# Inner channels of an expert in one block of 512 and three of 1024, on bias rows and a ring of six pieces

## The reference

```python
h = rms_norm(x, g_mix[l])
u = jnp.einsum('bsd,dc->bsc', h, w_in[l])
# three token mixers: pooling, convolution of 31 taps, forgetting attention of 8 heads
logf = jax.nn.log_sigmoid(f_logit)
c = cumsum(logf, axis=1)
s = einsum(q_i, k) * scale + (c_q - c_k)          # bias from the forget gates
s = where(kpos <= qpos, s, -inf); o = softmax(s) @ v
x = x + einsum(merged, w_out[l])
# channel mixer: layer 0 dense SwiGLU (2816 inner channels),
# layer 1 the two best of eight experts (3584 inner channels each)
out = out + gates[..., e:e + 1] * (silu(h @ w1[e]) * (h @ w3[e])) @ w2[e]
```

## Time and profile before

| | us |
|---|---|
| time, median of 3 runs | 1668.14 (1666.18 to 1669.09) |
| the profiled execution, its own time | 1673.39 |
| its span, first to last instruction | 1671.5 |
| TensorE busy in the span | 1634.1 (98%) |
| VectorE busy | 1290.0 (77%) |
| ScalarE busy | 1056.3 (63%) |
| mixer of layer 0, dense layer | about 0 to 230, 230 to 430 |
| mixer of layer 1, experts | about 430 to 645, 645 to 1671 |

### The profile page before, as it was taken

One profiled execution on the slowest core, in us unless ns is written; L12 is line 12 of the kernel. 1 busy time (PEld: TensorE's weight loads), 2 busy tenths in 40 slices (PEclk: granted clock), 3 DMA queues, 4 the chain that ended last, 5 costly groups with the idle time before them and its releaser, 6 DMA issues.

```text
span 1671.5 us, 25101 instructions
## 1 busy us (share of the span) xinstructions
PE 1634.1 (98%) x9644; PEld 1433.8 (86%) x9644; DVE 1290.0 (77%) x1097; ACT 1056.3 (63%) x908; POOL 61.9 (4%) x60
## 2 busy tenths in 40 slices
PE   7999989999899998999999999999999999999998
PEld 7998989999898897888888888888888888888887
DVE  5973764444697476897997998997988987987986
ACT  5444444454554454677777777777777777777775
POOL 0121100000012110000000000000000000000000
PEclk9999999999999998999999999999999999999999
DMA  9543455556454343799999999999999999999993
GB/s 335 167 146 106 127 167 171 191 175 200 126 170 133 103 133 120 258 377 369 327 374 354 344 371 340 358 372 334 365 371 333 363 375 334 359 377 334 359 377 132
DMA packets 231294, 452.48 MB, mean 271 GB/s; under 512 B 6992, under 2 KB 80720, under 8 KB 231120
## 3 DMA queue, kind: packets, MB, share of 16 engines
q1 hardware_dynamic: 231248, 451.82, 76.7%
HBM read 450.74 MB, written 1.05 MB: 270 GB/s over the span
## 4 chain that ended last, share of the span: by engine, by line
PE 93%; DVE 4%; ACT 2%; issue 1%; DMA 0%; ACTq 0%; DVEq 0%
PE bank L278 28%; PE bank L280 27%; PE bank L279 27%; PE bank L1292 2%; PE bank L1308 1%; DVE w_low L268 1%; PE bank L1326 1%; ACT w_high L264 1%; PE bank L1041 1%; PE bank L1129 1%; DVE h_full L628 1%; DVE rinv L618 0%; PE bank L1131 0%; PE bank L1148 0%; PE bank L1092 0%
## 5 line engine op out<-in xcount | busy, mean ns | idle before, releaser
L268 DVE TENSOR_TENSOR w_low<-raw,w_high 128x2048 fp32r<-128x2048 f32 x427 | 977.8, 2291 | 284.4 <-ACT w_high L264 283.2
L264 ACT ACTIVATE w_high<-raw 128x2048 fp32r<-128x2048 f32 x427 | 818.9, 1919 | 378.1 <-PE bank L280 376.7
L278 PE MATMUL bank<-w_high,hg_high 128*128 128x512 f32 x896 | 354.5, 396 | 0.7 <-issue 0.7
L280 PE MATMUL bank<-w_high,hg_low 128*128 128x512 f32 x896 | 350.1, 391 | 0.0
L279 PE MATMUL bank<-w_low,hg_high 128*128 128x512 f32 x896 | 349.3, 390 | 0.0
L278 PE MATMUL bank<-h_high,w_high 128*128 128x256 f32 x1056 | 301.8, 286 | 6.4 <-DVE h_low L623 4.8
L280 PE MATMUL bank<-h_high,w_low 128*128 128x256 f32 x1056 | 295.3, 280 | 0.0
L279 PE MATMUL bank<-h_low,w_high 128*128 128x256 f32 x1056 | 295.3, 280 | 0.0
L278 PEld LDWEIGHTS bank<-h_high,w_high 128*128 128x128 f32 x1056 | 200.8, 190 | 11.8 <-issue 9.4
L279 PEld LDWEIGHTS bank<-h_low,w_high 128*128 128x128 f32 x1056 | 199.1, 189 | 1.6 <-issue 1.4
L280 PEld LDWEIGHTS bank<-w_high,hg_low 128*128 128x128 f32 x896 | 168.6, 188 | 36.0
(11 more groups left out here) (242 smaller groups left out, 1586.6 us busy)
## 6 DMA issues: line engine op xcount, KB each, us to landing
raw<-exp_w SPq DMA_DIRECT2D x336, 1024.0 KB, 5.3
raw<-w_in SPq DMA_DIRECT2D x42, 1024.0 KB, 5.1
raw<-ffn_w SPq DMA_DIRECT2D x33, 1024.0 KB, 5.3
raw<-w_out SPq DMA_DIRECT2D x8, 1024.0 KB, 4.9
raw<-w_br_attn SPq DMA_DIRECT2D x4, 1024.0 KB, 5.0
raw<-w_br_pool SPq DMA_DIRECT2D x2, 1024.0 KB, 5.2
raw<-w_br_conv SPq DMA_DIRECT2D x2, 1024.0 KB, 4.9
cst<-consts SPq DMA_DIRECT2D x1, 1280.0 KB, 13.4
```

What stands on the lines that cost most here:

```text
L264: nc.scalar.activation(wh[c % SPLIT][:], raw[c % RAW][:], ACT.Copy).then_inc(s["high_done"], 1)
L268: nc.vector.tensor_tensor(wl[c % SPLIT][:], raw[c % RAW][:], wh[c % SPLIT][:].bitcast(F32), ALU.subtract).then_inc(s["split_done"], 1)
L278: pe.matmul(dst, lh, rh, start=start and i == 0, stop=False)
L280: last = pe.matmul(dst, ll, rh, start=False, stop=stop and i == len(terms) - 1)
```

## The change

It has three parts.

Bias rows: DVE writes the negated log forget gates of both token tiles into a zeroed tile nlf, twice (for high and low rows). PE sums them over the tokens with three fp32 matmuls, bias_sums, after piece 8. ACT and DVE make high and low rows of it in the tile crow. For each head one fp32r matmul with a broadcast column of sel8 adds the row to all queries; the term of the query falls out of the softmax. The mask is added in fp32r. POOL only zeroes tiles. The head's division moves up by one piece, and ten of the convolution's operations move ahead of other work.

Ring of six: w_low takes the memory of raw, so that DVE subtracts in place, and w_high has six tiles too. The load of piece c waits for used of piece c - 6; the high part waits for the load alone.

Wide expert blocks: block 0 of a job has 512 inner channels, and three more have 1024. Up pieces of a wide block have two row chunks by 1024 columns. A wide block takes two banks for w1 (0 and 5), two for w3 (1 and 6), two for the turns (4 and 7), and four down pieces. The work tiles of the experts lie over the tile h_full. The transposes of the permutation move to the start of the last block, and all of a job is written out on PE, ACT, DVE and SP, without an inner loop.

```diff
-RAW = 6
-SPLIT = 3
+RING = 6
...
+WIDE = 3
...
-GATHER_BANKS = (5, 6, 7, 0)
-TAPS_AT = {4: 6, 5: 6, 6: 1, 7: 1, 8: 1, 9: 1, 10: 8, 11: 8, 12: 8, 13: 8, 14: 7, 15: 7}
+GATHER_BANKS = (0, 5, 1, 6)
+COMBINE_BANKS = (5, 4, 6, 7)
+TURN_BANKS = (4, 7)
+TAPS_AT = {4: 6, 5: 6, 6: 1, 7: 1, 8: 1, 9: 1, 10: 8, 11: 8, 12: 6, 13: 5, 14: 5, 15: 4}
+TAPS_AHEAD = {12: 2, 13: 3, 14: 2, 15: 3}
...
-        raw = [sb(f"raw{i}", [P, PIECE]) for i in range(RAW)]
-        wh = [sb(f"w_high{i}", [P, PIECE], F32R) for i in range(SPLIT)]
-        wl = [sb(f"w_low{i}", [P, PIECE], F32R) for i in range(SPLIT)]
+        with ExitStack() as loaded:
+            raw = [loaded.enter_context(nc.sbuf_tensor(f"raw{i}", [P, PIECE], F32)) for i in range(RING)]
+        wl = [sb(f"w_low{i}", [P, PIECE], F32R) for i in range(RING)]
+        wh = [sb(f"w_high{i}", [P, PIECE], F32R) for i in range(RING)]
...
         def load_piece(sp, c, r, src, k):
-            if not (isinstance(r, int) and c < RAW):
-                sp.wait_ge(s["split_done"], num(c - RAW + 1, r))
-            sp.dma_start(fold(raw[c % RAW][:], k), src).then_inc(raw_in[c % RAW], 16)
+            if not (isinstance(r, int) and c < RING):
+                sp.wait_ge(s["used"], num(c - RING + 1, r))
+            sp.dma_start(fold(raw[c % RING][:], k), src).then_inc(raw_in[c % RING], 16)
 
         def split_high(act, c, r=0):
...
-            if not (isinstance(r, int) and c < SPLIT):
-                act.wait_ge(s["used"], num(c - SPLIT + 1, r))
...
+                def bias_sums():
+                    pe.wait_ge(s["nlf_in"], 2 * l + 2)
+                    pe.wait_ge(s["qk_root"], 4 * l + 3)
+                    pe.matmul(bank[6][0:64, 0:128], nlf[:, 0, :], C(C_UPTO), start=True, stop=True)
+                    pe.matmul(bank[6][0:64, 128:384], nlf[:, 0, :], C(C_UPTO, 2), start=True, stop=False)
+                    pe.matmul(bank[6][0:64, 256:384], nlf[:, 1, :], C(C_UPTO), start=False,
+                              stop=True).then_inc(s["bias_sum"], 1)
...
-                    pe.matmul(B[:, 0:128], q[:, 0:P], k[:, 0:P], start=True, stop=False)
-                    pe.matmul(B[:, 0:128], decay[:, h % 2, 0, :], C(C_AFTER), start=False, stop=False)
-                    pe.matmul(B[:, 0:128], ident, C(C_MASK), start=False, stop=True)
-                    pe.matmul(B[:, 128:384], q[:, P:S], k, start=True, stop=False)
-                    pe.matmul(B[:, 128:256], decay[:, h % 2, 2, :], C(C_AFTER), start=False, stop=False)
-                    pe.matmul(B[:, 128:384], decay[:, h % 2, 1, :], C(C_ONES, 2), start=False, stop=False)
-                    pe.matmul(B[:, 256:384], ident, C(C_MASK), start=False, stop=True).then_inc(s["scores"], 1)
+                    pe.matmul(B[:, 0:384], sel8[:, h:h + 1].to_broadcast([P, P]), crow[:], start=True, stop=False)
+                    pe.matmul(B[:, 0:128], identr[:], maskr[:], start=False, stop=False)
+                    pe.matmul(B[:, 256:384], identr[:], maskr[:], start=False, stop=False)
+                    pe.matmul(B[:, 0:128], q[:, 0:P], k[:, 0:P], start=False, stop=False)
+                    pe.matmul(B[:, 128:384], q[:, P:S], k, start=False, stop=True).then_inc(s["scores"], 1)
...
+                def up(c, r, banks, kn):
+
+                    for k0 in range(0, KC, kn):
+                        H, L = take_piece(pe, c, r, kn)
+                        for a, b in enumerate(banks):
+                            f = slice(512 * a, 512 * a + 512)
+                            ins = products(pe, bank[b][:], [
+                                (hgH[:, k0 + k, :], hgL[:, k0 + k, :], H[:, k, f], L[:, k, f]) for k in range(kn)],
+                                start=k0 == 0, stop=k0 + kn == KC)
                         ins.then_inc(s["used"], 1)
...
+                    for i in range(WIDE):
+                        if i == WIDE - 1:
...
+                        pe.wait_ge(s["m_silu"], r0 + (2 * i + 1))
+                        if i == 0:
                             pe.wait_ge(s["m_add"], j * 4 + 1)
...
+                        c = up(c, r0, (0, 5), 2)
...
+                        turn(r0 + (2 * i if i else 1), 2 if i else 1)
...
+                        c = up(c, r0, (1, 6), 2)
+                        c = down(c, r0, r0 + (2 * i if i else 1), 2 if i else 1, start=i == 0)
+                    turn(r0 + 2 * WIDE, 2)
                     pe.wait_ge(s["m_silu"], r0 + EXP_BLOCKS)
...
                     for g in range(4):
                         gather(g)
...
+                    down(c, r0, r0 + 2 * WIDE, 2, stop=True)
```

More of the change, by code:

```diff
@@ L220, in trunk @@
         x_in = [sem(f"x_in{m}") for m in range(4)]
-        raw_in = [sem(f"raw_in{i}") for i in range(RAW)]
+        raw_in = [sem(f"raw_in{i}") for i in range(RING)]
         def C(i, n=1):
@@ L560, in job @@
                     if not isinstance(j, int):
-                        for k in range(SPLIT):
+                        for k in range(3):
                             split_high(act, c + k, r0)
@@ L585, in experts @@
+                    split_high(act, c + 3, r0)
                 job(0)
@@ L976, in job @@
                     r0, c = j * EXP_BLOCKS, MOE0
-                    for k in range(SPLIT if isinstance(j, int) else 0, 4):
+                    for k in range(3 if isinstance(j, int) else 0, 4):
                         split_low(dve, c + k, r0)
@@ new lines, in job @@
+                    for i in range(WIDE):
+                        for k in range(0 if i else 2, 6):
+                            split_low(dve, c + k, r0)
+                            if i == 0 and k == 2:
+                                add_rows(j * 4, 1)
+                            elif i == 0 and k == 4:
+                                add_rows(j * 4, 2)
+                            elif i == 1 and k == 1:
+                                add_rows(j * 4, 3)
+                        for a in range(2 if i else 1):
+                            t_low(r0 + (2 * i + a if i else 1), a)
+                        for k in range(6, 10):
+                            split_low(dve, c + k, r0)
+                        for a in range(2):
+                            mult(r0 + (2 * i + 2 + a), j * JOB_PIECES + (c + 8), a)
+                        if i:
+                            split_low(dve, c + 10, r0)
+                        if i == 1:
@@ L1014, in experts @@
+                        c += 12 if i else 10
+                    split_low(dve, c, r0)
+                    split_low(dve, c + 1, r0)
+                    for a in range(2):
+                        t_low(r0 + 2 * WIDE + a, a)
+                    split_low(dve, c + 2, r0)
+                    split_low(dve, c + 3, r0)
                 job(0)
@@ L1294, in gather @@
                     ins.then_inc(s["m_gather"], 1)
-                def up(c, r, b):
-                    for half_ in range(2):
-                        H, L = take_piece(pe, c + half_, r, 4)
-                        ins = products(pe, bank[b][:], [
-                            (hgH[:, 4 * half_ + k, :], hgL[:, 4 * half_ + k, :], H[:, k, :], L[:, k, :]) for k in range(4)],
-                            start=half_ == 0, stop=half_ == 1)
-                        ins.then_inc(s["used"], 1)
-                def turn(count):
-                    pe.wait_ge(s["m_mult"], count)
-                    for k in range(4):
-                        ins = pe.transpose(bank[4][:, k * P:k * P + P], gu[:, k * P:k * P + P], ident)
-                    ins.then_inc(s["m_t"], 1)
@@ new lines, in turn, with down @@
+                def turn(count, halves):
+                    for a in range(halves):
+                        pe.wait_ge(s["m_mult"], count + a)
+                        for k in range(4):
+                            ins = pe.transpose(bank[TURN_BANKS[a]][:, k * P:k * P + P],
+                                               guE[:, 512 * a + k * P:512 * a + k * P + P], ident)
+                        ins.then_inc(s["m_t"], 1)
+                def down(c, r, count, halves, start=False, stop=False):
+                    for u in range(2 * halves):
+                        pe.wait_ge(s["m_low"], count + u // 2)
+                        H, L = take_piece(pe, c, r, 2)
@@ L1361, in job @@
+                    turn(r0 + 2 * WIDE, 2)
                     pe.wait_ge(s["m_silu"], r0 + EXP_BLOCKS)
-                    pe.wait_ge(s["m_add"], j * 4 + 4)
                     for g in range(4):
                         gather(g)
-                    pe.wait_ge(s["m_perm"], j * 4 + 6)
-                    for t in range(TT):
-                        ins = pe.transpose(bank[1][:, t * P:t * P + P], permC[:, t, :], ident)
-                    pe.wait_ge(s["m_gate"], j + 1)
-                    for t in range(TT):
-                        ins = pe.matmul(bank[1][:, S:S + 1], permC[:, t, :], gcol[:, t:t + 1], start=t == 0, stop=t == TT - 1)
```

258 lines of the change are left out of this document (140 added, 118 removed).

## The result

| | before | after |
|---|---|---|
| time, median of 5 runs, us | 1668.14 (1666.18 to 1673.0) | 1641.83 (1641.19 to 1649.6) |
| the profiled execution, us | 1673.39 | 1649.6 |
| its span, us | 1671.5 | 1647.8 |

After over before is 0.9853, with a 95% interval of 0.984 to 0.9867: 26.3 us less in the medians, 23.8 between the profiled executions. The forecast was 16.2 less (1652), with a range down to 1646. The kernel is faster as said, but by 10 us more than said, and outside the range.

The account below looks back on a forecast made before the run. TensorE's own issue was taken to set the time nearly everywhere. Bias rows saved 18.2 us less 2.0 for sums, wide blocks and ring 0, so 16.2 off the median 1668.14 gave 1652; range 1646 to 1663.

Parts of the forecast that it names:

- the ring was put at nothing: Ring of six, costed in the expert stage: stalls put at 0, with bounds of 0 and 1.5 us a job.
- part 1: Bias rows in the attention: 18.2 us saved over 16 heads, less 2.0 for added sums, so 16.2 us.
- So I add 0.1 on either side of the pair: Each head's scores: the two 64-row matmuls slow their neighbours, adding 0.2 us to a block of 1.63.
- the rival "more gain": Each head's scores: 64-row penalty paid only at row-mode changes, 0.2 us per head more, 3.2 in all, 1648.7; chance 0.14.
- Two mask matmuls at 0.22: Each head's scores: two 128-column fp32r mask matmuls cost 0.11 us each, priced from the gathers.
- a block of 1.5 to 1.7 us: Sign of being right: a head's new score matmuls take 1.5 to 1.7 us from first to behind the last.
- So 0 us, if nothing waits: Expert jobs with wide blocks: TensorE's work sums to 123.4 us against the period of 123.60, so no gain.
- Wide blocks at nothing: Expert stage: products stay 504 per job and joining turns saves no fixed part, so 0 us.
- The ring's margin: Expert pieces: 13.6 us of lead against a chain of 9.5, leaving 4.1 us, at worst 1.5.
- The rival "slower": Expert pieces: ring of six too short; a chain of 14.0 us costs 27 us, giving 1679; chance 0.08.
- No small stalls: Expert stage: stalls put at 0; the rival had about 1 us a job, 8 us, giving 1660, chance 0.12.
- The base: Whole kernel: the saving taken from the median 1668.14 us, not the profiled execution's 1673.39, giving 1652.

Follow-up runs that it names:

- the pair put apart again: The changed kernel with a mask product or two issued between each head's two q times k matmuls, so these are no longer adjacent: 1647.31 us, one execution.
- the narrow variant: The changed kernel with the expert blocks of the kernel before (seven of 512), bias rows and ring of six kept: 1643.57 us, ratio 0.985.
- three tiles: The changed kernel with the high part of piece c waiting again until TensorE has used piece c - 3: 1650.05 us, ratio 0.9889.
- The run with four pieces: The changed kernel with loads waiting so that four pieces instead of six are in use or under way: 1774.32 us, ratio 1.0636.
- five pieces: The changed kernel with each load waiting for one piece more, five instead of six in use or under way, six buffers kept: 1644.97 us.
- the masks apart: The changed kernel with the bias row split into 256 and 128 columns and one mask behind each: 1644.4 us, one execution.

## Why the prediction was wrong

Two steps failed, of nearly the same size: the price of the new score matmuls was too high (4.2 us over 16 heads), and the ring was put at nothing (4.4 us).

**Faster, and the mixers as the place: right.** The mechanism of part 1 was right; two of its terms were too dear. Counted as the forecast counts, its 2.77 a head for before was 2.78, and its 1.63 for the new block was 1.39.

- "So I add 0.1 on either side of the pair" on top of L1126 and L1129 at 1.04. That makes 1.24; the pair took 0.85, and its neighbours 0.1 more ahead and 0.07 behind, 1.01 or 3.7 us less over 16 heads. The 1.04 had half of each change of rows inside it already, four times over: the two matmuls stood apart in before. Putting them side by side saves 0.39 a head (the pair put apart again). This was the rival "more gain", which had 0.2 a head, 3.2 us, and a chance of 0.14. Its objection, that L1126 itself takes 0.41, was the sign for it: half of a change is paid in the 64-row matmul's own step.
- Two mask matmuls at 0.22. They took 0.06 and, without the change of rows behind it, 0.11 (0.20 with it): 0.05 less a head, 0.8 us. The gathers, from which the 0.11 came, are short products in a row; the first mask product follows one of 384 columns. Taken together, 1.14 x 16 = 18.2 was 22.4.

The 384-column product at 0.17 was right behind a product (103.74 to 103.91). So were the sums at 2.0 us for two layers. So part 1 was 20.4 and not 16.2, and the run with the bias rows alone gave 20.9. The sign that the prediction named, a block of 1.5 to 1.7 us, was missed too: it took 1.29.

**The ring at nothing: the other step that failed.** "So 0 us, if nothing waits" was worked out for the experts, and for them it held (123.60, 123.59). But the ring serves the mixers too. The prediction read 90 to 165 us, found TensorE busy 75.00 of 75, and took that for the whole mixer. From 165 to 215 it was busy 48.18 of 50. There the high part's wait for TensorE reached TensorE by way of DVE. The ring alone gave 4.4 us in the medians, with an interval that just includes nothing, and 4.5 within its two mixers; putting the wait back cost 2.7 there. By these runs 20.9 + 4.4 = 25.3 of the 26.3 us are accounted for; the rest is within the spread of the medians.

**Wide blocks at nothing: right**, by the narrow variant. They gave nothing, and seem to have made the job dependent on the high part running ahead (124.08 with three tiles).

**The ring's margin: right, and smaller than said.** The prediction had 13.6 us of lead against a chain of 9.5. The run with four pieces shows a turn of 13.3 with the use of 2.7 in it, so the chain with its queueing is 10.6, an estimate; five pieces were just too few now and then (0.5 us a job), and six leave about one piece. The rival "slower" would have been right at a ring of four: it cost 132 us over the changed kernel.

**No small stalls:** no wait of TensorE for an expert piece, 39 instruction packets against 35.

**The base.** The saving was set against the median, 1668.14. That was sound, as both kernels have the same two groups of executions and both medians lie in the lower one.

## What to carry to other kernels

Read every stretch in which a changed resource is used, not only the ones that the change is about: a shared ring or a helper is worth what it does in all its callers, and a busy share of 98% over the span leaves room for 4 us of waits in a place one didn't look. Price a matmul from a row with the same neighbours: its step depends on the length of the one ahead and on whether the number of rows changes, and a change is paid half in the matmul ahead of it and half in the one behind. When a kernel is compared with another, compare stage by stage: a clock that comes back 3.5 us earlier, or a dense layer in its other step, is not the change's work. When matmuls use half the rows, issue those of the two halves side by side, and place the group where its banks have been read.

## What the hardware showed that was not expected

- A stream of 256-column products, each with its own weights, steps at 113.3 or at 117.8 ns, at the same granted clock of 1.00, and keeps to one of the two for nearly a whole dense layer (7 us over its 1584 products). What decides isn't settled; it differed between executions of one kernel. In the mixers both steps occur within one execution.
- Matmuls on rows 0 to 63 and 64 to 127 start 7 ns apart and run beside each other: two heads' passes took the 0.32 us of one.
- A change between 64 and 128 rows costs about 0.2 us (0.39 a head for two), half in the pass ahead of it (0.20 instead of 0.11) and half in the pass behind (0.21).
- A 128-column product behind one of 256 or 384 columns steps at 0.06 us instead of 0.11, with the same weights behind it (the two masks) or others (the masks apart).
- At the start of the experts the granted clock was 0.50 for 13.7 us in some runs and 10.2 in others, worth 1.6 us in the first job.
